# First modulation slices of 128 and 256 features instead of 256, in a decoder layer on one Trainium2 core

## What is computed

```
mod = silu(c) @ w_ada + b_ada                  # 6 x 1024 numbers; c has 1024
shift1, scale1, gate1, shift2, scale2, gate2 = split(mod, 6)
h = rms_norm(x, norm1_g) * (1 + scale1) + shift1
proj = h @ w_in                                # q, k, v, indexer qi / ki / wi, pooling, gates
```

## Time and profile before

| | us |
|---|---|
| median of 3 runs | 735.27 (735.15 to 735.4) |
| profiled execution, its own time | 735.97 |
| its span, first to last instruction | 734.1 |
| mean granted TensorE clock | 0.994 |

### The profile page before, as it was taken

How to read it: one execution, slowest core, us unless ns; L and a number is a source line. 1 busy time by engine, 2 the same in 40 slices (tenths; PEclk the granted TensorE clock), 3 DMA queues, 4 the chain that set the end, 5 groups by cost and what they waited for, 6 DMA issues and landing times.

```text
span 734.1 us, 9316 instructions
## 1 busy us (share of the span) xinstructions
PE 717.5 (98%) x3440; PEld 577.4 (79%) x3440; DVE 382.5 (52%) x706; ACT 307.7 (42%) x507; POOL 299.8 (41%) x159
## 2 busy tenths in 40 slices
PE   5899999999999999999999999999999999999997
PEld 3667688877776778887898888887888888888886
DVE  3458899964375506788955444545443432004002
ACT  6316532567577633352636334344334333121120
POOL 1001448826232325574315434434444434435440
PEclk9899999999999999999999999999999999999999
DMA  9993321311231226486095243244243233042401
GB/s 317 357 392 115 108 80 58 115 58 59 69 103 53 64 66 258 164 307 208 1 315 151 81 115 105 68 115 114 58 116 96 76 114 114 31 144 86 144 0 58
DMA packets 87306, 92.73 MB, mean 126 GB/s; under 512 B 2275, under 2 KB 69599, under 8 KB 87263
## 3 DMA queue, kind: packets, MB, share of 16 engines
q1 hardware_dynamic: 84927, 83.23, 35.5%
q10 hardware_dynamic: 2336, 8.92, 3.3%
HBM read 90.05 MB, written 2.10 MB: 126 GB/s over the span
## 4 chain that ended last, share of the span: by engine, by line
PE 81%; DVE 14%; ACT 1%; DMA 1%; SPq 1%; issue 1%; DVEq 0%; ACTq 0%
PE bank L1575 33%; PE bank L1595 21%; PE bank L1584 16%; PE bank L1645 4%; DVE work L1312 3%; DVE top L1309 3%; PE bank L1839 1%; PE bank L1827 1%; PE bank L1807 1%; DMA ada_first<-in_w_ada_dram 1%; PE bank L1627 1%; DVE macc_rows L1174 1%; DVE full L1490 1%; DVE pmean L1343 1%; DVE pmean L1339 1%
## 5 line engine op out<-in xcount | busy, mean ns | idle before, releaser
L704 POOL TENSOR_TENSOR wsplit<-stage,wsplit 128x1024 fp32r<-128x1024 f32 (+1 forms) x113 | 259.3, 2297 | 387.3 <-ACT wsplit L788 328.0
L1575 PE MATMUL bank<-hT,wsplit 128*128 128x512 f32 (+1 forms) x1120 | 257.5, 382 | 0.4 <-DVE hT L1498 0.4
L1575 PEld LDWEIGHTS bank<-hT,wsplit 128*128 128x128 f32 x1120 | 203.0, 188 | 41.9 <-issue 1.7
L788 ACT ACTIVATE wsplit<-stage 128x1024 fp32r<-128x1024 f32 (+2 forms) x121 | 120.0, 994 | 249.8 <-PE bank L1584 165.2
L1584 PE MATMUL bank<-hT,wsplit 128*128 128x512 f32 (+1 forms) x560 | 134.6, 382 | 0.0
L1595 PE MATMUL bank<-wsplit,guT 128*128 128x512 f32 x528 | 119.8, 389 | 0.0
L1584 PEld LDWEIGHTS bank<-hT,wsplit 128*128 128x128 f32 x560 | 101.5, 188 | 19.9 <-POOL wsplit L704 0.3
L1595 PEld LDWEIGHTS bank<-wsplit,guT 128*128 128x128 f32 x528 | 99.1, 188 | 20.6
L1533 DVE SCALAR_TENSOR_TENSOR yb<-bank,conv,yb 128x511 f32<-128x511 f32 (+1 forms) x44 | 33.0, 749 | 65.1 <-ACT yb L1108 64.3
L1533 DVE SCALAR_TENSOR_TENSOR ya<-bank,conv,ya 128x511 f32<-128x511 f32 (+1 forms) x44 | 33.0, 750 | 59.6 <-ACT ya L1108 58.8
L1458 DVE TENSOR_TENSOR tmp_last<-bank,gate_row 128x512 f32<-128x512 f32 x8 | 5.5, 688 | 101.7 <-PE bank L1595 101.7
(11 more groups left out here) (193 smaller groups left out, 754.3 us busy)
## 6 DMA issues: line engine op xcount, KB each, us to landing
stage<-in_w_up_dram SPq DMA_DIRECT2D x44, 512.0 KB, 5.2
stage<-in_w_in_dram SPq DMA_DIRECT2D x14, 1024.0 KB, 5.2
stage<-in_w_down_dram SPq DMA_DIRECT2D x10, 1024.0 KB, 5.0
ada_first<-in_w_ada_dram SPq DMA_DIRECT2D x16, 512.0 KB, 9.5
ada_mid<-in_w_ada_dram ACTq DMA_DIRECT2D x8, 1024.0 KB, 7.9
ada_row<-in_w_ada_dram SPq DMA_DIRECT2D x8, 512.0 KB, 11.3
stage<-in_w_out_dram SPq DMA_DIRECT2D x4, 1024.0 KB, 7.2
ada_last<-in_w_ada_dram SPq DMA_DIRECT2D x4, 1024.0 KB, 11.0
```

The lines of the kernel that those rows point to most:

```text
L704: pool.tensor_tensor(unit_split(n, 1), unit_source(n), unit_split(n, 0).bitcast(F32), ALU.subtract).then_inc(low, 1)
L788: me.did(act.activation(unit_split(n, 0), unit_source(n), ACT.Copy), high)
L1575: pe.matmul(out_bank[:, tokens], hi[:, k, :], rhs[:, part, k, tokens], start=k == 0 and part == 0, stop=False)
```

## The change

The slices of the first modulation get 128, 128, 128, 128, 256 and 256 features (`WIDE`), so that slice 0 serves feature block 0 alone. Narrow slices are loaded by two DMAs of 512-byte runs. Weight items hold one feature block each (eight items for the first products instead of four). The biases and gains are loaded by ACT's queue, four before the Silu and two behind the first root; the taps are loaded by SP behind item 1. Sixteen transposes of `ident` into bank 7, which nobody reads, follow the transpose of c on PE. The transpose of `rows` now goes to `OB`, ahead of the token transposes; the taps are transposed inside the first products (`tap_turn`). Token blocks 0 to 6 are transposed as before, with `first_sums(0)` ahead of the last tile; block 7 is transposed into `OB` behind the first columns (`last_turn`). The square of token tile 1 moves from ACT to DVE, and DVE copies c before ACT's Silu. `xn` lies elsewhere, so that the load of slice 4 waits for `last_turn`. The copies of the banks are interleaved with the steps of slice 0, and `full1` of block 0 reads its bank directly.

```diff
-ROW_LOADS = 11
+ROW_LOADS, TAP_LOADS = 6, 3
+EARLY = (("qi", 0), ("qi", 1), ("kw", 0), ("q", 1), ("q", 2), ("q", 3), ("q", 0))
...
+WIDE = (1, 1, 1, 1, 2, 2)
+NQ = len(WIDE)
+AT = tuple(sum(WIDE[:q]) for q in range(NQ))
+SLICE_OF = tuple(q for q in range(NQ) for _ in range(WIDE[q]))
...
-        xn = place("xn", [P, NT, D], F32, hT_at)
+        xn = arena("xn", [P, NT, D], F32, 62)
...
-        ada_first = [arena(f"ada_first{q}", [P, KD, S], F32, (16, 32, 62, 89)[q]) for q in range(KQ)]
+        ada_first = [arena(f"ada_first{q}", [P, KD, 2 * WIDE[q] * P], F32, (16, 32, 62, 89)[AT[q] // 2] + AT[q] % 2 * 8)
+                     for q in range(NQ)]
...
+                wide = WIDE[q] * P
+                if AT[q] == 4:
+                    sp.wait_ge(last_t, 1)
+                if WIDE[q] == 1:
+                    for j in range(2):
+                        c0 = j * D + AT[q] * P
+                        sp.dma_start(ada_first[q][:, :, j * P:(j + 1) * P], ada[:, :, c0:c0 + P]
+                                     ).then_inc(ada_in[q][0], 16)
+                    return
...
-                        c0 = j * D + 2 * q * P
-                        sp.dma_start(ada_first[q][:, ks, 2 * j * P:2 * (j + 1) * P], ada[:, ks, c0:c0 + 2 * P]
+                        c0 = j * D + AT[q] * P
+                        sp.dma_start(ada_first[q][:, ks, j * wide:(j + 1) * wide], ada[:, ks, c0:c0 + wide]
...
-                if n == KQ - 1:
+                if n == 1:
+                    load_taps()
+                if n == KD - 1:
...
+            for r, src in ((V_ADA, b_ada), (V_NORM1, norm1_g), (V_NORM2, norm2_g), (V_POOL, pool_scale)):
+                v = src[0].rearrange("(k p) -> k p", p=P)
+                act.dma_start(rows[r:r + v.shape[0], 0, :], v).then_inc(rows_in, 16)
+            act.wait_ge(c_kept, 1)
+            me.did(act.activation(csil[:, :], csil[:, :], ACT.Silu), c_silu)
             me.did(act.activation(tstat[:, 2, 0:1], ones[:, 0:1], ACT.Sqrt))
-            for t in range(NT):
+            def token_squares(t):
                 act.wait_ge(x_in[t], 16)
-                me.did(act.activation(junk[:, t % 2, :], xtok[:, t, :], ACT.Square,
-                                      accum_out=tstat[:, 0, t:t + 1]), x_sum)
+                me.did(act.activation(junk[:, 0, :], xtok[:, t, :], ACT.Square, accum_out=tstat[:, 0, t:t + 1]), x_sum)
                 me.settle()
-                me.did(act.activation(tstat[:, 2, t:t + 1], tstat[:, 0, t:t + 1], ACT.Sqrt, bias=eps[:, 0:1],
+            def token_roots(t0, t1):
+                me.did(act.activation(tstat[:, 2, t0:t1], tstat[:, 0, t0:t1], ACT.Sqrt, bias=eps[:, 0:1],
                                       scale=1.0 / D), root_ok)
+            token_squares(0)
+            token_roots(0, 1)
+            for r, src in ((V_Q, q_norm_g), (V_K, k_norm_g)):
+                act.dma_start(rows[r:r + 1, 0, :].rearrange("p (a d) -> p a d", a=2),
+                              src.unsqueeze(1).to_broadcast([1, 2, HD])).then_inc(rows_in, 16)
+            act.wait_ge(x_square, 1)
+            token_roots(1, 2)
+            token_squares(2)
+            token_roots(2, 3)
+            token_squares(3)
+            token_roots(3, 4)
+            def x_copy(k):
+                me.did(act.activation(xT[:, k, :], banks[k][:, :], ACT.Copy), x_kept[0])
+            def h_high(k):
+                act.wait_ge(n_ok, k + 1)
+                me.did(act.activation(hT[:, 0, k, :], full1[:, k % 2, :], ACT.Copy), h_hi)
+            def row_sum(q):
+                n = 2 * WIDE[q] * P
+                act.wait_ge(sums_ok, q + 1)
+                me.did(act.activation(rowsum[:, 0:n], OB[:, 0:n], ACT.Copy), row_ok)
             act.wait_ge(x_t, NT)
-            for k in range(0, KD, 2):
-                me.did(act.activation(xT[:, k, :], banks[k][:, :], ACT.Copy), x_kept[0])
-            for q in range(KQ):
-                act.wait_ge(sums_ok, q + 1)
-                me.did(act.activation(rowsum[:, :], OB[:, :], ACT.Copy), row_ok)
-                high_parts(2 * q + 1)
-                for k in (2 * q, 2 * q + 1):
-                    act.wait_ge(n_ok, k + 1)
-                    me.did(act.activation(hT[:, 0, k, :], full1[:, k % 2, :], ACT.Copy), h_hi)
-                high_parts(2 * q + 2)
+            x_copy(4)
+            row_sum(0)
+            x_copy(2)
+            high_parts(1)
+            x_copy(6)
+            h_high(0)
+            act.wait_ge(last_t, 1)
+            me.did(act.activation(xT[:, KD - 1, :], OB[:, :], ACT.Copy), last_kept)
+            for q in range(1, NQ):
+                row_sum(q)
+                for k in range(AT[q], AT[q] + WIDE[q]):
+                    high_parts(k + 1)
+                    h_high(k)
...
+            def first_full(k):
+                if k >= 2:
+                    dve.wait_ge(h_lo, k - 1)
+                if k % 2 == 0 and k:
+                    dve.wait_ge(x_kept[0], (0, 2, 1, 3)[k // 2])
+                if k == KD - 1:
+                    dve.wait_ge(last_kept, 1)
+                source = xT[:, k, :] if k else banks[0][:, :]
+                me.did(dve.tensor_scalar(full1[:, k % 2, :], source, gs[:, 0, k:k + 1], mod[:, k:k + 1],
+                                         ALU.mult, ALU.add), n_ok)
...
+            dve.wait_ge(c_t, 1)
+            me.did(copy_of(csil[:, :], banks[2][:, 0:KD]), c_kept)
+            dve.wait_ge(consts, 13)
+            me.did(dve.reciprocal(invn[:, :], invn[:, :]))
             dve.wait_ge(c_silu, 1)
-            dve.wait_ge(consts, 13)
             me.did(copy_of(cpad[:, :, 0], csil[:, :]), c_pad)
-            me.did(dve.reciprocal(invn[:, :], invn[:, :]))
+            dve.wait_ge(x_in[1], 16)
+            me.did(dve.tensor_tensor_reduce(junk[:, 1, :], xtok[:, 1, :], xtok[:, 1, :], 1.0, 0.0, ALU.mult, ALU.add,
+                                            tstat[:, 0, 1:2]), x_square)
...
+                if t == 0:
+                    vectors()
+            def x_copy(k):
+                me.did(copy_of(xT[:, k, :], banks[k][:, :]), x_kept[1])
             dve.wait_ge(x_t, NT)
-            for k in (KD - 1, 1, 3, 5):
-                me.did(copy_of(xT[:, k, :], banks[k][:, :]), x_kept[1])
-            vectors()
-            for q in range(KQ):
+            x_copy(3)
+            first_vectors(0)
+            first_full(0)
+            x_copy(5)
+            x_copy(1)
+            first_low(0)
+            low_parts(1)
+            for q in range(1, NQ):
                 first_vectors(q)
-                for k in (2 * q, 2 * q + 1):
-                    if k % 2 == 0:
-                        dve.wait_ge(x_kept[0], k // 2 + 1)
-                    if k >= 2:
-                        dve.wait_ge(h_lo, k - 1)
-                    me.did(dve.tensor_scalar(full1[:, k % 2, :], xT[:, k, :], gs[:, 0, k:k + 1], mod[:, k:k + 1],
-                                             ALU.mult, ALU.add), n_ok)
-                for k in (2 * q, 2 * q + 1):
+                ks = range(AT[q], AT[q] + WIDE[q])
+                for k in ks:
+                    first_full(k)
+                if q == 2:
+                    tap_vectors()
+                for k in ks:
                     first_low(k)
                     low_parts(k + 1)
-                for k in ((), (), (0, 1, 2, 3, 4), (5, 6, 7))[q]:
+                for k in {4: (0, 1, 2, 3, 4), 6: (5, 6, 7)}.get(AT[q], ()):
...
-            pe.wait_ge(c_silu, 1)
-            for t in range(NT):
-                pe.wait_ge(xn_ok, t + 1)
-                for k in range(KD):
-                    mm = pe.transpose(banks[k][:, t * P:(t + 1) * P], xn[:, t, k * P:(k + 1) * P], ident[:, :])
-                mm.then_inc(x_t, 1)
+            for _ in range(16):
+                pe.transpose(banks[7][:, 0:P], ident[:, :], ident[:, :])
+            def row_turn():
+                pe.wait_ge(rows_in, 16 * ROW_LOADS)
+                pe.transpose(OB[:, 0:V_END], rows[0:V_END, 0, :], ident[0:V_END, 0:V_END]).then_inc(rows_t, 1)
+            def tap_turn():
+                pe.wait_ge(taps_in, 16 * TAP_LOADS)
+                pe.wait_ge(first_mod, 3)
+                pe.transpose(OB[:, 0:P], rows[:, 1, :], ident[:, :])
+                left = (TAPS + 1) * 2 * KF - P
+                pe.transpose(OB[:, P:P + left], rows[0:left, 2, :], ident[0:left, 0:left]).then_inc(taps_t, 1)
+            def last_turn():
+                pe.wait_ge(first_mod, 1)
+                for t in range(NT):
+                    mm = pe.transpose(OB[:, t * P:(t + 1) * P], xn[:, t, (KD - 1) * P:KD * P], ident[:, :])
+                mm.then_inc(last_t, 1)
             def first_sums(q):
+                n = 2 * WIDE[q] * P
                 if q == 0:
                     pe.wait_ge(c_pad, 1)
-                    pe.wait_ge(x_kept[1], 1)
+                    pe.wait_ge(vec_ok, 1)
                 else:
                     pe.wait_ge(first_mod, q)
+                if q == 1:
+                    pe.wait_ge(last_kept, 1)
```

(102 more changed lines are left out.)

36 lines of the change are left out of this document (10 added, 26 removed).

## The result

| | before | after |
|---|---|---|
| median | 735.34 us | 745.29 us (744.04 to 747.45, 4 runs) |
| profiled execution, span | 734.1 us | 743.6 us |
| ratio of the times | | 1.0139, 95% interval 1.0125 to 1.0152 |

What follows compares the result with a forecast made beforehand. TensorE was taken as the bound, with a 20.73 us head of small steps and a body of matmuls. Head -0.98, body +1.65 and clock -2.54 summed to -1.87 us: 733.4 us on the median, range 731.3 to 737.6.

Steps and rivals of the forecast that it cites:

- the landing of the q and k gains: Head: second gain load issued at about 7.75 us, landing 2.76 us at most, all rows there by 10.5 us.
- rival 3: Head: gains land late; with 5.2 us of landing 735.8 us, with slow transposes 737.1 us; chance 12%.
- the transposes at 0.14 us: Head: with the clock up, seven token transposes take 0.95 us and keep pace with xn.
- the gate rows: PE's body: fifth row summed at 56.8 us, 1.1 us late against 1.6 us PE has in hand, so hidden, barely.
- The cost of the finer slices: PE's body: more sums and columns there, 1.33 us, plus two tap transposes, 0.3 us; +1.65 us in sum.
- The clock under the first products: First 21 products: they come before the clock falls, so 2.54 us return.
- rival 2: First products run at 1.2 GHz all the same: 735.9 us alone, 8%; 737.2 us together with Rival 1, 13%.
- The head behind the last transpose: Copies, row sums, columns, vectors and high parts up to the first product: 3.7 us, ending at 19.75 us.
- X: Head: the moment the last seven token transposes end, forecast at 16.0 us.
- The first slice: Head: the 1 MB slice lands at 13.5 us, before the sums want it, so the transfer leaves the chain.
- ACT's four issues ahead of the Silu: Head: four row loads issued on ACT move the Silu's start from 3.81 to 4.45 us.
- Rival 1: Head: unread transposes warm nothing that lasts, token transposes take 0.22 us each, +1.3 us, 734.7 us; alone 15%.

Runs made afterwards that it cites:

- e6: Changed kernel with gate rows loaded early, gains still late, the transpose of the rows moved behind the third token tile and its copy behind the fourth xn; 736.45 us, ratio 1.0012.
- e7: e3 with the transpose of the rows moved as in e6; 736.02 us, ratio 1.0002.
- e3: Changed kernel with both edits, q and k gains issued early and gate rows one weight block earlier; 735.48 us, ratio 0.9997.
- e1: Changed kernel with the q and k gains issued by ACT ahead of the Silu instead of behind the first root; 742.1 us, ratio 1.0079.
- e2: Changed kernel with the gate row loads queued behind weight block 6 instead of weight block 7; 739.86 us, ratio 1.0054.
- e5: e3 without the change's sixteen unread transposes; 735.53 us, ratio 0.9997.
- e8: Changed kernel with the q and k gains loaded by four plain loads instead of two with a repeated source, same place; one execution, 746.93 us.
- e11: e5 with all six row loads at the head of SP's queue, ahead of x, instead of on ACT's queue; one execution, 738.46 us.
- e9: e7 with ten more unread transposes between the transposes of the last block and the first product; 734.54 us, ratio 0.9984.
- e4: Kernel before the change, plus only 12 unread transposes between the first columns and the first product; 734.01 us, ratio 0.9972.
- e10: e9 with two narrow slices instead of four (128, 128, 256, 256, 256 features); 735.23 us, ratio 0.9991.

## Why the prediction was wrong

The sum said -1.87 us and the span grew by 9.5. Step by step:

- **The step that failed first: the landing of the q and k gains, taken at 2.76 us from `crow`.** It took 5.4. `crow` was issued in the same moment as the first tile of x (0.75 and 0.74 us), into engines that had moved nothing yet: 0 GB/s up to 1.5 us and 89 in the next half microsecond. The gains were issued into engines that moved 323 to 324 GB/s (7.5 to 12 us). The upper bound of 5.2 us, from large loads, was the right row, and rival 3, built on it, had this mechanism, but ended at 737.1. The first product came at 23.75 us instead of 19.75, of which 2.5 us are this landing and about 1.5 the token transposes at 0.22 us each behind it, the clock having fallen to 0.50 between 10 and 12 us while PE waited. The forecast had the transposes at 0.14 us, and rival 3 took slow ones for an extra. The landing is not the only thing that makes them slow: in e6 and e7, where PE does not wait for the rows, 21 of them took 4.16 and 4.09 us.
- **The step that failed most: the gate rows, "hidden, barely".** The forecast had the weight block issued 26.6 us into the products and the fifth row summed 10.4 us behind that. It was issued at 28.1, and the sum was over 13.9 us behind: the first row took 6.2 us from its issue, with idle engines to start from, and five sums followed at DVE's own pace. The columns came 1.3 us later than forecast as well (DVE could have taken them up at 61.0 us, 37.2 us into the products; forecast were 55.7 us and 35.95). So DVE was late by 1.1 + 1.5 + 3.5 - 1.3 = 4.8 us, and PE had 1.6 in hand: 3.2, measured 3.24. Nor did the forecast carry the stall on to what comes behind it, a longer wait for `kiT` (1.2 us) and PE's clock behind that wait (1.3 us). No rival had this place, though the text had named how thin its cover was.
- **The cost of the finer slices** was the right term at the wrong size, 2.6 us for 1.65. The half slices (1.34 us) and the taps (0.30) cost what was forecast; the breaks in the run of products were not in the sum.
- **The clock under the first products** came back in the profiled execution, worth 2.3 us where 2.54 were forecast. That was in part luck: of the nine profiled executions with this stretch of 3.7 us and no spares in it only two, those of the changed kernel and of e3, kept the clock; e1, e2, e5, e6, e7, e8 and e11 lost it. A shorter thin stretch is not enough, and rival 2 was the likelier outcome.
- **The head behind the last transpose**: forecast 3.7 us from X to the product, measured 3.75 (20.00 to 23.75). Right, though ACT's own terms as given add up to 2.93 us and not 2.85. The first slice was forecast to land at 13.5 us and landed at 12.9 in e9, where PE waits for it.
- **ACT's four issues ahead of the Silu** were priced at 0.64 us and cost nothing: they were issued while the table was being loaded, from 1.41 to 2.81 us, and the Silu ran at 4.02.
- **Rival 1** (spares that warm nothing that lasts) was right about the sixteen: with the gains late they end 5.6 us before PE has work again, and with early gains (e3 and e5) their absence can't be measured in the median.

## What to carry to other kernels

Price a small load by the traffic that it will travel in, not by one that set out into idle engines, and let nothing large stand behind its wait that does not need it: moving the wait alone was worth 0.4% here, moving the load 0.6%. When queue items become finer, look at what stands behind them in the queue: a prefetch of three items now reached half as far, and loads that waited for nothing stood behind one that waited for DVE. Where TensorE has a thin stretch just before dense work, a few unread transposes right there kept its clock (e4, e9, e10), and sixteen more than 10 us earlier did not.

## What the runs showed of the hardware

A load of one row of 512 bytes took 1.7 us ahead of all other traffic and 4.5 to 6.3 us within it, with the same form or as plain loads. On ACT's queue, which had only other small loads in it, it took that long all the same; no run shows it on SP's queue in the midst of x. Eight ready loads of 512 KB, issued behind a weight block to engines that had just stood idle, had the first of them landed only after 6.2 us, in which some 1.7 MB were moved (278 GB/s from 53 to 59 us), where the weight block and that load together have 1.0. The clock's fall before the first products differed between kernels that are alike up to there: it stayed up in e3 and fell in e1, e2, e5, e6 and e7, with the same instructions of PE in the stretch ahead. The column of the granted clock reads 1.00 from the start of every trace, but transposes of one shape took 0.22 to 0.23 us each before a first rise and 0.14 after it, so up to the first recorded change the pace of the instructions tells the clock, not the column.
